# Gated delta rule: the norm of q folded into the norm of the output, its sum of squares moved from TensorE to GpSimd

## The reference, cut to what matters

```
q = l2norm(silu(conv(p_q))) * 128 ** -0.5      # l2norm(x) = x * rsqrt(sum(x*x) + 1e-6)
k = l2norm(silu(conv(p_k)))
# per v head and direction, chunks of tokens; decay from cumulative gates
qk    = (q @ k.T) * decay ;  q_dec = q * exp(gc)
v_new = u_i - w_i @ s
o_i   = q_dec @ s + qk @ v_new                 # linear in q, token by token
o     = o_forward + o_backward
o     = rmsnorm(o, g_norm)                     # o * rsqrt(mean(o*o) + 1e-6) * g
y     = (o * silu(z)) @ w_out
```

## Time and profile before

| | us |
|---|---|
| median of 3 runs | 3300.11 (3296.35 to 3301.86) |
| the profiled execution's own time | 3295.26 |
| its span, first to last instruction | 3293.5 |
| PE matmuls busy | 3108.8 (94%) |
| DVE busy | 1745.3 (53%) |
| ACT busy | 1522.9 (46%) |
| POOL busy | 775.7 (24%) |

### The profile page before, as it was taken

How to read it: one execution, slowest core, us unless ns; L and a number is a source line. 1 busy time by engine, 2 the same in 40 slices (tenths; PEclk the granted TensorE clock), 3 DMA queues, 4 the chain that set the end, 5 groups by cost and what they waited for, 6 DMA issues and landing times. The chain is left out here.

```text
span 3293.5 us, 56323 instructions
## 1 busy us (share of the span) xinstructions
PE 3108.8 (94%) x22057; PEld 2038.3 (62%) x22057; DVE 1745.3 (53%) x3545; ACT 1522.9 (46%) x3283; POOL 775.7 (24%) x588
## 2 busy tenths in 40 slices
PE   5878999999999999999999999796999999999998
PEld 2346777777777764455545565443777777777753
DVE  1136666666666652244442344344667767766632
ACT  3135555555555541145532444333556555555521
POOL 0033433333343220001101011003343434343300
PEclk9689999999999999999999999998999999999999
DMA  9911211221121027012302111202122212121135
GB/s 375 321 56 44 70 51 56 60 60 56 48 73 56 29 70 264 3 53 63 132 18 49 33 46 41 82 11 72 49 62 64 64 52 72 52 75 53 43 118 191
DMA packets 224099, 261.97 MB, mean 80 GB/s; under 512 B 19418, under 2 KB 158948, under 8 KB 223716
## 3 DMA queue, kind: packets, MB, share of 16 engines
q1 hardware_dynamic: 223844, 258.46, 24.6%
HBM read 239.15 MB, written 19.27 MB: 78 GB/s over the span
## 5 line engine op out<-in xcount | busy, mean ns | idle before, releaser
L894 PE MATMUL ps<-hT,W 128*128 128x512 f32 (+1 forms) x2656 | 997.4, 506 | 3.2 <-DVEq L192 2.0
L894 PEld LDWEIGHTS ps<-hT,W 128*128 128x128 f32 x2656 | 470.4, 192 | 200.8 <-issue 171.6
L1319 DVE CAST_PREDICATED arena<-mask,ps 128x384 bf16<-128x384 uint32 x448 | 252.6, 564 | 201.7 <-PE ps L963 166.2
L1144 ACT CAST arena<-ps 128x384 bf16<-128x384 f32 x384 | 167.0, 482 | 339.0 <-PE ps L950 338.0
L2355 PE MATMUL ps<-arena 128*128 128x512 f32 x712 | 309.5, 592 | 2.6 <-SPq L192 2.4
L1321 DVE CAST_PREDICATED arena<-mask,ps 128x384 bf16<-128x384 uint32 x448 | 250.2, 558 | 0.0
L2355 PEld LDWEIGHTS ps<-arena 128*128 128x128 f32 x712 | 133.9, 190 | 166.4 <-issue 161.7
L1990 PE MATMUL ps<-hT,W 128*128 128x512 f32 (+1 forms) x608 | 218.2, 493 | 0.8 <-DMA W<-in_att_w_in 0.5
L1431 POOL TENSOR_TENSOR arena<-arena,cst 128x768 f32<-128x768 f32 x64 | 117.1, 1852 | 386.6 <-DVE arena L1288 384.0
L1300 DVE SCALAR_TENSOR_TENSOR arena<-arena,vec 128x770 f32<-128x770 f32 (+1 forms) x192 | 196.2, 1022 | 6.8
L961 PEld LDWEIGHTS ps<-arena 128*128 128x128 bf16 x2304 | 153.1, 98 | 42.4 <-issue 32.5
(11 more groups left out here) (279 smaller groups left out, 6112.5 us busy)
## 6 DMA issues: line engine op xcount, KB each, us to landing
arena<-in_ada_w SPq DMA_DIRECT2D x24, 2048.0 KB, 19.5
W<-in_gdn_w_in SPq DMA_DIRECT2D x95, 512.0 KB, 4.0
arena<-decay_sums SPq DMA_DIRECT2D x64, 384.0 KB, 4.1
W<-decay_rows SPq DMA_DIRECT2D x64, 384.0 KB, 5.1
arena<-in_gdn_w_out SPq DMA_DIRECT2D x32, 512.0 KB, 10.6
W<-in_gdn_w_out SPq DMA_DIRECT2D x30, 512.0 KB, 3.5
arena<-gated SPq DMA_DIRECT2D x32, 384.0 KB, 8.0
gated<-arena SPq DMA_DIRECT2D x24, 384.0 KB, 2.3
```

Source lines behind the costliest of these rows:

```text
L894: mm = pe.matmul(ps[:, b, 0:t1 - t0], w[:, i, :], env.hT[:, i, t0:t1], start=(i == 0), stop=(i == KD - 1))
L1144: act.copy(half_cols(Xb[d], s, d), ps[:, 2 * d, 0:384].rearrange("p (c b s) -> p c b s", c=NT, s=s)).then_inc(*inxe.up(m, lv, d))
L1319: dve.copy_predicated(half_cols(Mb[d], s, d), wide(env.m4[:, d, lv]), src_m).then_inc(*inm.up(m, lv, d, "m"))
```

## The change

For q tiles (n odd) the normalisation is left out: no x0, x1 on PE, no Ln and Exp on ACT, no product on DVE. q stays raw; G and QD wait for SiLU (`sx`) only. POOL computes q2 = q * (eps*128*128), then q2 = q2 * q, in a buffer of its own (two of them, used in turn), and after the squares of the output it adds q2 to them, before the matmul by ones. The bias of the output's Ln changes from eps to eps*eps*128. The temporary `offneg` goes; L1400 becomes a scalar_tensor_tensor with the same result. k tiles are as before, and so is the plan of the even slots.

```diff
-        dve.memset(env.epsc[:, 1:2], EPS * P)
+        dve.memset(env.epsc[:, 1:2], EPS * EPS * P)
...
-        normed = (["x1"] if short else ["x0", "x1"]) * (tile and n > -2)
+        normed = ["x0", "x1"] * (tile and n > -2 and n % 2 == 0)
...
-                    if starts:
+                    if starts and n % 2 == 0:
                         pe.wait_ge(nrm.sem, nrm.at(n))
+                    elif starts:
+                        pe.wait_ge(sx.sem, sx.at(n, 1))
...
-                sc, e = (1.0 / P, 0) if use[0] == "o" else (1.0, 0) if n % 2 == 0 else (float(P), 1)
+                sc, e = (1.0 / P, 1) if use[0] == "o" else (1.0, 0)
...
-                    dve.tensor_tensor(v.KK, v.KK, v.offneg.unsqueeze(1).broadcast_to([P, NT, P]), ALU.mult).then_inc(*kkn.up(n // 2 + 1))
+                    dve.scalar_tensor_tensor(v.KK, env.ident.unsqueeze(1).broadcast_to([P, NT, P]), -1.0, v.KK,
+                                             ALU.add, ALU.mult).then_inc(*kkn.up(n // 2 + 1))
...
-                if p == 14 and n in TILES:
-                    t = v.k if n % 2 == 0 else v.q
+                if p == 14 and n in TILES and n % 2 == 0:
                     dve.wait_ge(xrs.sem, xrs.at(n))
-                    lo = q_from(n)
-                    dve.tensor_tensor(t[:, lo:T], t[:, lo:T], v.sq[:, lo:T], ALU.mult).then_inc(*nrm.up(n))
+                    dve.tensor_tensor(v.k, v.k, v.sq, ALU.mult).then_inc(*nrm.up(n))
...
             if n in TILES:
-                t = v.k if n % 2 == 0 else v.q
                 pool.wait_ge(sx.sem, sx.at(n, 1))
-                pool.wait_ge(og.sem, og.at(n - 1, 0))
                 lo = q_from(n)
-                pool.tensor_tensor(v.sq[:, lo:T], t[:, lo:T], t[:, lo:T], ALU.mult).then_inc(*sqx.up(n))
+                if n % 2 == 0:
+                    pool.wait_ge(og.sem, og.at(n - 1, 0))
+                    pool.tensor_tensor(v.sq, v.k, v.k, ALU.mult).then_inc(*sqx.up(n))
+                else:
+                    q2 = v.q2[(n + 1) // 2 % 2][:, lo:T]
+                    pool.tensor_scalar(q2, v.q[:, lo:T], EPS * P * P, None, ALU.mult).then_inc(*qsc.up(n))
+                    pool.wait_ge(qsc.sem, qsc.at(n))
+                    pool.tensor_tensor(q2, q2, v.q[:, lo:T], ALU.mult).then_inc(*sqx.up(n))
             if m in U:
-                pool.wait_ge(nrm.sem, nrm.at(n if n % 2 else n - 1))
+                pool.wait_ge(sx.sem, sx.at(n if n % 2 else n - 1, 1))
...
             if n in U:
                 pool.wait_ge(rue.sem, rue.at(n, NT - 1, 1, "o"))
-                pool.wait_ge(nrm.sem, nrm.at(n))
+                pool.wait_ge(nrm.sem, nrm.at(n // 2 * 2))
                 pool.wait_ge(og.sem, og.at(n - 1, 0))
                 ot = v.OT[:, n % 2, LO:T]
-                pool.tensor_tensor(v.sq[:, LO:T], ot, ot, ALU.mult).then_inc(*osq.up(n))
+                pool.tensor_tensor(v.sq[:, LO:T], ot, ot, ALU.mult).then_inc(*osf.up(n))
+                pool.wait_ge(osf.sem, osf.at(n))
+                pool.wait_ge(sqx.sem, sqx.at(n // 2 * 2 - 1))
+                pool.tensor_tensor(v.sq[:, LO:T], v.sq[:, LO:T], v.q2[n // 2 % 2][:, LO:T], ALU.add).then_inc(*osq.up(n))
```

More of the change, by code:

```diff
@@ L632, in gdn_phase @@
     NEG, KDEC, DCH, COL = range(4)
-    v = carve(env, [("pad", (2, PADW)), ("acc", (2, CONVW)), ("q", (T,)), ("k", (T,)), ("kS", (T,)), ("sq", (T,)),
+    v = carve(env, [("pad", (2, PADW)), ("acc", (2, CONVW)), ("q", (T,)), ("k", (T,)), ("kS", (T,)), ("sq", (T,)), ("q2", (T,), 2),
                     ("vtok", (NT, P)), ("ktok", (NT, P)), ("sz", (2, T)), ("KK", (NT, P)), ("QK", (NT, P)),
-                    ("OT", (2, T)), ("S", (2, P)), ("R", (2, P)), ("V", (2, P)), ("VK", (2, P)), ("offneg", (P,)),
+                    ("OT", (2, T)), ("S", (2, P)), ("R", (2, P)), ("V", (2, P)), ("VK", (2, P)),
                     ("NAT", (NT, P), 2), ("MF", (NT, P), 2), ("MT", (NT, P), 2), ("QKD", (NT, P), 2),
@@ L653, in gdn_phase @@
     t_ld = seq("t_ld", [(k,) for k in ("dt0", "dt1", "al0", "al1")], 16)
-    t_set = seq("t_set", [(k,) for k in ("sgn", "neg", "zero", "wpad", "r1", "r0f", "r0b", "pad", "xb0", "xb1", "off", "nid", "hot0", "hot1")])
+    t_set = seq("t_set", [(k,) for k in ("sgn", "neg", "zero", "wpad", "r1", "r0f", "r0b", "pad", "xb0", "xb1", "nid", "hot0", "hot1")])
     t_pad = seq("t_pad", [("w",)])
@@ L694, in gdn_phase @@
     sqx = seq("sqx", [(n,) for n in TILES])
-    xrs = seq("x_rs", [(n,) for n in TILES])
-    nrm = seq("nrm", [(n,) for n in TILES])
+    xrs = seq("x_rs", [(n,) for n in TILES if n % 2 == 0])
+    nrm = seq("nrm", [(n,) for n in TILES if n % 2 == 0])
     kkn = seq("kkn", [(h,) for h in range(GH)])
@@ L706, in gdn_phase @@
     rue = seq("rue", [(m, s, d, k) for m in U for s in range(NT) for d in BOTH for k in "so" if (s < NT - 1 if k == "s" else out_at(s))])
+    qsc = seq("q_scaled", [(n,) for n in TILES if n % 2])
+    osf = seq("osf", [(m,) for m in U])
     osq = seq("osq", [(m,) for m in U])
@@ L1250, in vector @@
         dve.memset(Xb[1], 0.0).then_inc(*t_set.up("xb1"))
-        dve.tensor_scalar(v.offneg, env.ident, -1.0, None, ALU.add).then_inc(*t_set.up("off"))
         dve.tensor_scalar(v.nidb, env.ident, -1.0, None, ALU.mult).then_inc(*t_set.up("nid"))
```

## The result

The changed kernel took 3323.76 us (median, 3320.86 to 3332.52) beside 3300.56 for the kernel before on the same chip: a ratio of 1.0082, 95% interval 1.0060 to 1.0105. It is slower by 0.6 to 1.05%, some 23 us, where 12 were forecast. The profiled execution took 3320.86 us with a span of 3319.1, against the 3295.3 and 3293.5 of before, so it has 25.6 us to explain.

A forecast was written before the change was run, and what follows sets the result against it. PE was taken to bound the kernel nearly everywhere, other engines close behind at two places. Layer 0 -9.0+10.0, layer 3 -2.1+3.5, slots -1 +3.5, slots 14 and 15 +6.4 gave +12.3 on 3300.1: 3312.4 us, range 3297 to 3324.

The forecast's parts named there:

- the even-to-odd boundary: Even slot's end: POOL's addition holds up DVE's L1342, so PE's L1031 comes 1.43 us later; layer 3, 0.5.
- The addition's price: POOL's addition of q2 to the output's squares: 1.82 us at 768 columns, 1.27 at 512.
- The waits in slots 14 and 15: PE's first fill also waits for POOL's addition: 1.88 us a slot in layer 0, 1.33 in layer 3; +6.4.
- PE's price for the two sums: Odd slot of layer 0: PE's two removed float32 matmuls by ones, 0.43 and 0.86 us, 1.29 together.
- the first branch of rival C: Odd slots: level products and copies, not PE, are the bound, so removal brings nothing; C 3323.5 us, chance 0.14.
- For tensor_scalar I take the copy's 0.83 as nearest: POOL's scaling of q in layer 0 odd slots: 0.83 us like a one-input copy, ends 0 and 1.82.
- the fill between L1321 and the next L950 absorbs it: Layer 0 odd slots: DVE's 1.1 us delay beside POOL's chain costs nothing, as 2.6 us of fills cover it.
- the second branch of rival C: Odd slots: q2 takes 1.82 us, QD ends 1 us later, delaying L1342, convolution and L973; C 3323.5 us, chance 0.14.
- the 11 us forecast for the removal: Odd slots: PE's removed sums save 9.0 us in layer 0 and 2.1 in layer 3.
- So -1.29 in full: Each steady odd slot of layer 0 keeps the whole saving of 1.29 us; seven slots, -9.0 us.
- the 0.3 forecast: Layer 3 odd slots: POOL's chain holds L1342, so PE's 0.86 us saving becomes 0.3; seven slots, -2.1 us.
- Slot -1: QD, behind q2, meets DVE's convolution, which ends 2.4 us later in layer 0, 1.1 in layer 3; +3.5.

The follow-up runs named there:

- late q2: Changed kernel with POOL doing both QD first and q2 only behind the convolution of v in the same slot; ratio to before 1.0053.
- the removal alone: Changed kernel without q2 and without POOL's addition, so q's norm is left out altogether; ratio to before 0.9984.
- the three together: Changed kernel with q2 behind the convolution, the addition moved between the next slot's low parts (heads 0 to 12), and the fill plan of before; ratio 1.0001.
- KK alone: Kernel before with only L1400 made a scalar_tensor_tensor on the identity; one time, 3306.3 us.

## Why the prediction was wrong, point by point

The direction, slower, and the mechanism of the even-to-odd boundary were right; the size was off by half, 12 us for 23, and the time, 3323.8, was at the range's upper end of 3324. The slots themselves grew by 29.7 us; that the time shows 23 is owed to phases that the change doesn't touch.

*Right.* The addition's price: 1.82 and 1.27 us taken, 1815 and 1272 ns measured. The boundary: 1.43 a pair forecast in layer 0, 1.42 measured by leaving the addition out and by moving it; 0.5 in layer 3, 0.48. The waits in slots 14 and 15: 1.88 and 1.33 forecast, 1.89 and 1.34 measured. That their total came to 6.9 us for 6.4 is luck in slot 14 of layer 0: the forecast had neither the 1.25 us of a wait for ACT that the later start hides, nor the 1.69 us of the lower clock. L1400 at nothing: so. PE's price for the two sums, 1.29 us: 1.28 in the kernels with nothing else in the way. That also settles the first branch of rival C for layer 0, and the rule of the Trainium skill behind it ("Trainium Kernel Development and Optimization", section Performance Expectations), which calls matmul busy time a bad metric and that of the weight loads a good one: with weight loads busy 61% and matmuls 93%, taking 1.29 us of matmuls out of a slot made it 1.28 us shorter, so here the matmuls' time was the measure. The four weight loads that went with them are 0.19 us each, 0.76 in all, and would not give 1.28. In layer 3's odd slots the branch holds in part: with all of POOL's new work gone 0.43 of the 0.86 us was kept, and by the wait rows the rest went into the wait for DVE's copies at step 15, much as the forecast had it.

*Failed: "For tensor_scalar I take the copy's 0.83 as nearest".* This is the step that mattered most. tensor_scalar took 2.13 us (1.49 at 512 columns), outside the bounds given, 0 and 1.82. It is not the work of a collision: seven of eight in layer 0 took 2.13, and in late q2, where it stands elsewhere, all eight did. I took the two-input product as the upper end for a one-input operation; nothing in the trace said so. POOL's chain then ended not 1.2 us into L1342 but 2.98 us into it (505.77 to 508.75), and L1342 took 3.79 us. The prediction had "the fill between L1321 and the next L950 absorbs it"; it absorbed a part, and 0.77 and 0.85 us a pair were left. (495.0 + 6.3 is 501.3 and not the 501.5 of the forecast; nothing hangs on it.) Both the kernel without the scale and the one with q2 late give these numbers, one by taking work away, one by order alone. With slots -1 and 13 this is some 13 us of the profiled 29.7. It is the second branch of rival C, which named this chain at a q2 of 1.82 us and got 0.14. Its sum, 3323.5, met the measured time for a partly wrong reason: it lost the 11 us forecast for the removal, where in truth a part of these was lost to the plan, and other phases hid 4 us of the rest.

By the Trainium skill's line on one-input work ("GPSIMD Engine Reference", section 4.1) q2 would have been 0.64 us, an estimate; the trace disagrees, and the measurement decides: 2.13.

*Failed: "So -1.29 in full".* The diff changes the list that the fills are planned from, and I moved only the fills behind step 11 in thought. The planner moved earlier ones as well: o0, o1 and V0.0 came into one step, and V0.0 waits for the bank that ACT is still reading. In layer 0 this costs 0.84 us an odd slot (0.84 as well from the removal alone to the three together, 62.93 to 62.09). In layer 3 the new plan is the better one, by 0.45. There the removal alone kept 0.43 of 0.86; the 0.3 forecast was to hold with q2 in place, but q2 took another 0.85, so removal and q2 together gave +0.42 an odd slot instead of -0.3.

*Slot -1.* 3.5 us were forecast for both layers, 4.1 came: 3.56 in layer 0 for 2.4, 0.56 in layer 3 for 1.1. Moving q2 gives back 2.9 of layer 0's. The clock has a share here. Rows for slot -1 of layer 0, before and after:

```profile
231.60:280.50 48.90, 36.14 (x409) 27.27 (x406) 32.06 (x47) 28.52 (x55) 21.37 (x16) 0.86 0.20 53
```
```profile
229.50:281.90 52.40, 35.28 (x402) 27.45 (x399) 33.55 (x46) 26.69 (x52) 22.73 (x17) 0.77 0.18 50
```

The mean granted clock fell from 0.86 to 0.77, time at the lower level, 1.2 GHz, from 13.6 to 23.9 us, while PE's busy share went from 74 to 67%. A part can be told apart: KK alone, whose slot -1 is that of before, took 49.60 us with 20.5 us at the lower level, so 0.7 us of the 3.6 are clock that the change need not have caused. Late q2 took 49.52 and the removal alone 49.45, both with 20.5 us. The other 2.9 go with q2 ahead of QD, its 3.4 us more at the lower level included; how much of them is collision and how much clock was not taken apart. Nor was slot -1 of layer 3 in the last kernels, 46.8 us instead of 44.5 with 23.9 us at the lower level instead of 20.5: it stays open.

*The sum in new figures.* Per pair, layer 0: -1.29 (sums) +1.42 (addition) +0.84 (plan) +0.77 (q2) = +1.74, measured 1.76 to 1.79. Layer 3: -0.43 +0.48 +0.85 = +0.90, measured 0.89. Slot 13 has the same odd-slot terms. Against the forecast, layer 0's slots 0 to 13 add 11.5 us (q2 and the plan), layer 3's 4.8 (q2), slots -1 0.6 and slots 14 and 15 0.5; with the 12.3 forecast that is the 29.7 measured.

## What to carry to other kernels

Work moved to a helper engine is paid where it stands beside another engine's instructions and holds them up, not where its busy share says: list which instructions of the other engines will stand beside it, by the clock, and try its order before its size. An operation that no row shows has no upper end in its neighbours' rows; time it alone before it is placed ahead of something that matters. A wait that grows on the bounding engine can also cost it its clock behind the wait, as in slot 14. And where a list of fills is planned, taking one out re-times those ahead of it too: read the new plan for which buffer follows which, since a removal kept 1.28 us under one plan and 0.44 under another.

## What the runs showed of the hardware that was not expected

GpSimd's tensor_scalar on float32 is slower than a product of two tensors: 2.13 us against 1.82 for 128x768, 1.49 against 1.27 for 128x512, while a copy takes 0.83. A product of a tensor with itself takes 1.47 and 1.04 where nothing holds it up.

A DVE instruction with two SBUF inputs ended only 0.8 us after the GpSimd instruction beside it, as if it had started then: L1345, 1.82 us for two alone, 3.25 beside one addition and 3.79 beside two QD, which themselves took 4.32 instead of 3.59. This follows the forecast at the boundary, but its size at 3.79 was new. The Trainium skill ("SBUF — State Buffer", section "Who interferes with whom") describes the pair of ports that the two engines share as held for a whole instruction; this case's rows agree, and with both queues full the two engines took whole instructions in turn, QD, L1345, QD, L1345, in the four rows above. One DVE instruction with a single tensor input was held up too, in slot -1 beside a QD that began with it; before, the same tensor_scalar (L1297) took 0.61 us:

```profile
255.28 2.22 DVE L1300 TENSOR_SCALAR arena<-arena,vec 128x770 f32<-128x770 f32 x1
```
